# Latent pages of the late decode steps: four gathered by GpSimd instead of two

## The reference

```python
def step(carry, phys):                       # phys: one page per sequence
    c_blk = cache_ckv[layer, phys]           # 128 x 256 latent rows
    kp_blk = cache_kpe[layer, phys]          # 128 x 32 rotary keys
    kn_blk, v_blk = _decompress(c_blk, w_ukv, g_kn)   # keys are RMS-normed per head
    return _merge(carry, _attn_partial(qn, qp, kn_blk, kp_blk, v_blk, None)), None
carry, _ = lax.scan(step, init, page_table.T)         # softmax merged page by page
```

## Time and profile before

| | |
|---|---|
| time, median of 3 runs | 1275.35 us (1275.25 to 1277.68) |
| the profiled execution's own time | 1276.86 us |
| its span, first to last instruction | 1275.1 us |
| busy: PE / DVE / ACT / POOL | 94% / 57% / 33% / 20% of the span |
| mean granted TensorE clock | 0.984 of full speed |
| late steps' gathers on GpSimd (L489) | 48, of 944 ns |
| page transfers issued by SP (L441) | 208 |

### The profile page before, as it was taken

How to read it: one execution, slowest core, us unless ns; L and a number is a source line. 1 busy time by engine, 2 the same in 40 slices (tenths; PEclk the granted TensorE clock), 3 DMA queues, 4 the chain that set the end, 5 groups by cost and what they waited for, 6 DMA issues and landing times. The chain is left out here.

```text
span 1275.1 us, 23690 instructions
## 1 busy us (share of the span) xinstructions
PE 1202.1 (94%) x8783; PEld 661.3 (52%) x8783; DVE 732.2 (57%) x1801; ACT 426.5 (33%) x1041; POOL 257.4 (20%) x294
## 2 busy tenths in 40 slices
PE   6999999989999999999989988999999999989898
PEld 3545677745565565655434445555444444454343
DVE  4000437955667666774768787888676667430331
ACT  3000354323343333342444343333444444210310
POOL 0000134711011121234412340001323232000000
PEclk9999999999999999997999999999999999999999
DMA  6413112123232222351453226532576544101000
GB/s 219 168 55 87 35 33 67 53 59 80 66 81 67 76 73 77 84 115 42 124 143 88 76 74 171 168 80 74 153 184 172 139 122 123 50 1 38 17 21 33
DMA packets 205236, 114.45 MB, mean 90 GB/s; under 512 B 152977, under 2 KB 196433, under 8 KB 204994
## 3 DMA queue, kind: packets, MB, share of 16 engines
q1 hardware_dynamic: 198482, 96.56, 27.7%
q0 software_dynamic: 4352, 10.49, 3.3%
q10 hardware_dynamic: 2288, 5.89, 1.3%
HBM read 75.79 MB, written 4.07 MB: 63 GB/s over the span
## 5 line engine op out<-in xcount | busy, mean ns | idle before, releaser
L563 PE MATMUL PS<-wk,c_T 128*128 128x512 f32 x1024 | 494.5, 612 | 13.5 <-DVE c_T L673 12.4
L563 PEld LDWEIGHTS PS<-wk,c_T 128*128 128x128 f32 x1024 | 180.3, 193 | 207.8 <-issue 162.8
L686 DVE TENSOR_REDUCE ssq<-PS 128x8 f32<-128x512 f32 x256 | 176.3, 689 | 169.7 <-ACT PS L609 156.8
L609 ACT ACTIVATE PS<-PS 128x512 f32<-128x512 f32 x256 | 150.3, 587 | 271.8 <-PE PS L563 245.0
L1557 PE MATMUL PS<-xnT,w_ring 128*128 128x276 f32 x416 | 101.0, 400 | 0.0
L1395 PE MATMUL PS<-w_ring,xnT 128*128 128x424 f32 x256 | 96.4, 534 | 0.9 <-DVE xnT L1041 0.9
L673 DVE STREAM_TRANSPOSE c_T<-blocks 128x512 f32<-128x512 f32 x126 | 88.3, 701 | 3.7 <-DMA blocks<-c_ring 3.2
L1557 PEld LDWEIGHTS PS<-xnT,w_ring 128*128 128x128 f32 x416 | 77.8, 190 | 20.6 <-issue 4.1
L489 POOL DMA_INDIRECT c_ring<-in_cache_ckv,token_rows x48 | 45.3, 944 | 182.1 <-PE PS L547 174.8
L480 POOL DMA_INDIRECT r_ring<-in_cache_kpe,group_rows x64 | 62.0, 969 | 92.3 <-DVE r_T L681 68.0
L1395 PEld LDWEIGHTS PS<-w_ring,xnT 128*128 128x128 f32 x256 | 48.8, 194 | 45.5 <-issue 45.4
(11 more groups left out here) (535 smaller groups left out, 1725.3 us busy)
## 6 DMA issues: line engine op xcount, KB each, us to landing
blocks<-c_ring SPq DMA_DIRECT2D x504, 64.0 KB
c_ring<-in_cache_ckv SPq DMA_DIRECT2D x208, 128.0 KB, 2.2
w_ring<-in_w_in SPq DMA_DIRECT2D x4, 1696.0 KB, 12.4
w_ring<-in_w_in SPq DMA_DIRECT2D x9, 512.0 KB, 5.1
w_o<-in_w_out SPq DMA_DIRECT2D x8, 512.0 KB, 4.9
w_g<-in_w_ple_gate SPq DMA_DIRECT2D x8, 512.0 KB
xn<-in_x_prompt SPq DMA_DIRECT2D x4, 512.0 KB, 10.9
w_ring<-in_w_in SPq DMA_DIRECT2D x2, 1024.0 KB, 6.1
```

The lines of the kernel that those rows point to most:

```text
L563: mm = pe.matmul(PS[:, NORM[v % 2], :], c_T[:, u % 2, k, t * P:(t + 1) * P], wk[:, k], start=(k == 0), stop=(k == 1))
L609: nc.scalar.activation(PS[:, NORM[v % 2], :], PS[:, NORM[v % 2], :], ACT.Square).then_inc(no_sb, 1)
L686: dve.tensor_reduce(ssq[:, u % 2, t * H:(t + 1) * H], PS[:, NORM[v % 2], :].rearrange("p (h c) -> p h c", h=H), AX.X, ALU.add).then_inc(re ...
```

## The change

From step 40 on GpSimd gathers all four pages, and SP reads no page numbers, waits for no place in the ring and issues no page transfer for these steps: only the rearranging transfers are left to it. Both halves of a late step then wait for all four gathers (64 on `late_in`). The table `token_rows` is filled for all four pages of the late steps. `slot_taken` is dropped everywhere, and with it one semaphore bump per step on SP.

```diff
-                    for x in range(GT // 2 if gathered(u) else GT)]
+                    for x in range(0 if gathered(u) else GT)]
...
-            if half == 1 and gathered(u):
-                nc.sync.wait_ge(late_in[u % 2], 32 * ((u - GATHERED) // 2 + 1))
+            if gathered(u):
+                nc.sync.wait_ge(late_in[u % 2], 64 * ((u - GATHERED) // 2 + 1))
...
-                if u >= RING:
+                if u >= RING and not gathered(u):
                     sp.wait_ge(vv_ps, u - RING + 1)
-                    sp.sem_inc(slot_taken, 1)
...
                     pool.wait_ge(vv_ps, u - RING + 1)
                     pool.wait_ge(hi_sb, u - 2)
-                    for x in (2, 3):
+                    for x in range(GT):
...
-                    late = [a.rearrange("p (j b x) -> p j b x", b=BS, x=GT)[:, :, GATHERED // STEPS:, 2:4] for a in (token_rows[:], pages[:])]
+                    late = [a.rearrange("p (j b x) -> p j b x", b=BS, x=GT)[:, :, GATHERED // STEPS:, :] for a in (token_rows[:], pages[:])]
```

More of the change, by code:

```diff
@@ L411, in build @@
         NFIRST = CONST["lnscale"][0] + 1
-        (slot_taken, k_ps, k_sb, tn_sb, rp_ps, no_ps, no_sb, red_sb,
+        (k_ps, k_sb, tn_sb, rp_ps, no_ps, no_sb, red_sb,
          ri_sb, scale_sb, scale_ps, np_sb, top_sb, al_sb, eq_sb, ew_ps, ew_sb, vv_ps, acc_sb, dve_a) = kept_sems(*(
-            "slot_taken k_ps k_sb tn_sb rp_ps no_ps no_sb red_sb "
+            "k_ps k_sb tn_sb rp_ps no_ps no_sb red_sb "
             "ri_sb scale_sb scale_ps np_sb top_sb al_sb eq_sb ew_ps ew_sb vv_ps acc_sb dve_a").split())
```

## The result

The changed kernel takes 1280.55 us (median of 7 runs, 1277.74 to 1283.98), the kernel before 1275.59 in the same comparison (7 runs, 1273.01 to 1277.68). The ratio is 1.0039 [1.0022, 1.0056]: slower by 5 us, 2.8 to 7.1. I had forecast 1273.7 and a range up to 1277.5. The forecast was wrong in sign.

A forecast was written before the change was run, and what follows sets the result against it. SP's rounds were taken to lengthen five tail steps above a 9.04 us floor. -2.4 + 0 gave 1274.5 us against the profiled 1276.86; for unprofiled runs, the middle of 1273.0 and 1274.5, 1273.7, range 1272.0 to 1277.5.

The forecast's parts named there:

- SP's round and the floor: Tail: SP's round falls from 8.87 to 5.33 us; PE, ACT and DVE need 9.04 us a step anyway.
- the 2.4 us of the tail: Tail: what five steps longer than 9.04 us lose in total, to be repaid by the change.
- the new wait's room: Late steps: half b ready 1.46 us before it is wanted, 0.48 with a 3.9 us landing; cost taken as 0.
- P + 6.73: Late steps: predicted start of SP's blocks, in us from P, the start of the row's first gather.
- The weight loads: Tail: ten 512 KB loads start beside the third and fourth gather; cost taken as 0.
- my own limit: Late steps: room ends at a gather landing of 4.4 us, or blocks starting later than P + 8.2.
- the 1.93 of the sum: Late steps: time in us from the end of SP's eight issues to DVE's start, assumed to stay as before.
- rival 1: Tail: weight loads collide with the gathers, 2.5 to 5 us lost, total 1276.2 to 1278.7 us; chance 0.15.
- steps that lengthen in pairs: Tail: one of the signs listed as showing the forecast wrong; no size given.
- only the key gather ... its reader is two steps away: POOL, late steps: all that is queued behind the two added gathers, starting 2.50 us later.
- Rivals 2 and 4: Late steps: fourth gather late every step, 1283 to 1286 us (0.08); DVE holding GpSimd up, about 1287 (0.02).
- Rival 3: Long steps: measured runs lose more there than the profiled one, so more gain, 1271 to 1272.8 us; chance 0.14.

The follow-up runs named there:

- halves_43: Changed kernel with a semaphore for each half's gathers and GpSimd gathering from step 43 instead of 40: 1276.34 us, ratio 0.9997; run again 1274.85 us, 0.9973.
- with late loads: Changed kernel with all ten weight loads issued behind the last step instead of one per late step: 1276.88 us, ratio 1.0013 to the kernel before.

## Why the prediction was wrong

**Right: SP's round and the floor.** SP left the chain. From 1018.86 on, behind the loads, the tail of the changed kernel goes at 9.05 us a step, and the 2.4 us of the tail exist: halves_43 gets them (-2.6 at equal clock, twice, with 2.2 in the steps of the second one). But 0.4 of the 2.4 belongs to a step of 9.40 to 9.42 that the changed kernel, too, has in that place (1009.44 to 1018.86): a pause on DVE itself ahead of the square sums. The kernel before, then the changed one:

```profile
1007.34 0.69 DVE L686 TENSOR_REDUCE ssq<-PS 128x8 f32<-128x512 f32 x1 [0.41 <-DVE nmax L712]
...
1009.89 0.69 DVE L685 TENSOR_REDUCE ssq<-PS 128x8 f32<-128x512 f32 x1 [0.40 <-issue]
```

I had counted this step as SP's, by the wait of 0.39 us that follows there in the kernel before; that wait is gone, but the pause stays and the step is as long. It went only where the gathered steps began at 43, and in these three kernels a pause of the same size stands in the step at 806 to 810 instead. Whether it is the same one, the runs don't show.

**Right: the new wait's room, undisturbed.** Behind the loads, in the row at 1032.86, the blocks start at P + 6.62 against the P + 6.73 worked out, which leaves the room of 1.5 us.

**Wrong, the first failed step: "The weight loads ... I take 0: the slowest of 208 page transfers took 3.9 us, which still fits."** I had seen that the loads would start at P + 3.0, beside the third and fourth gather. But the 3.9 us came from an order in which SP issued pages and loads itself, one behind the other. It could not bound a gather with a load beside it. In the row at 949.07 the fourth gather, issued at 952.83, landed some 4.9 us later (957.75 less 0.06), not 2.9 to 3.9. By my own limit a landing of 4.4 us ends the room. The limit itself was generous: the row at 930.32 had its blocks begin at P + 7.51, and half b was still 0.80 us late. Its eight issues took 6.12 us and not 5.33, and DVE started 2.7 us behind their end and not the 1.93 of the sum; in the other late rows that was 2.4 to 2.6. This part is not shown to be the loads' doing: with late loads one row has the same, blocks at P + 6.88 and half b 0.56 us late, with no load near it. The cost was the rest of the tail's excess, 4.4 less 0.4, 4.0 us; with late loads 0.6 to 0.7 of it stay, so the loads make about 3.4. This was rival 1, with a chance of 0.15: right in place and direction, and also in size for the tail (2.5 to 5 us). The forecast of the total had no room for it, because the sum took the loads at 0. What I took for "steps that lengthen in pairs" was every second step.

**Wrong, what no step or rival had: the steps beside the attention.** I let the added gathers start at the tail and asked only whether POOL had time. But the first row of four begins at 846.48 us, three steps ahead of the tail, where the prompt's attention shares TensorE and DVE. There, in all but one of the steps with a row of five, DVE gets TensorE's results 0.5 to 0.9 us late, straight or by way of ACT, 1.6 to 2.2 us in all. The prediction's sentence on what is queued behind the added gathers ("only the key gather ... its reader is two steps away") asked who waits for the gather and not whom the gather disturbs. Why TensorE's count comes late then is not settled. What is shown is when it happens: with a fifth transfer at the end of the row, be it keys or a page, and not with four.

**Together:** -2.0 repaid, +4.0 in the tail, +1.6 beside the attention: +3.6 us, where the stretch measures +3.7, the equal-clock comparison +3.9, and the runs +5.0 (2.8 to 7.1).

**Rivals 2 and 4** are excluded: rows without loads are in time, but for the one with late loads, and no gather exceeded 958 ns. Rival 3's further gain isn't there: halves_43 stops at 9.04 a step.

## What to carry to other kernels

When a step is taken off a queue, everything behind it in that queue starts earlier; here ten 512 KB loads moved from behind the page transfers to beside the gathers that replaced them, and that alone cost 3.4 us, more than the 2.4 that were to be gained. A transfer's slowest landing in the old order is no bound for the new one; leave room, or wait for each part of the data by itself: the semaphore for each half took the late steps out with the loads still beside the gathers. And look at every stage in which the new code runs, not only at the one it was made for: beginning three steps later saved about 2 us.

## What was unexpected of the hardware

A row of five GpSimd gathers beside the prompt's attention went with a late count from TensorE in 14 rows of 15, mostly 0.5 to 0.75 us of DVE's time, twice by way of ACT, though TensorE had done the work in time; three rows of four had none. A 128 KB gather, fourth of a row, lands about 2.8 us behind its start undisturbed (P + 6.62, less 3.76 and 0.06, as SP's next issue shows it) and up to 4.9 us with a 512 KB load beside it.
